# The inverses of an RWKV-7 mixer: whole 128x128 blocks, or packed 64x64 diagonal blocks and a corner by two products

## The reference

```python
def step(S, inp):
    w_t, k_t, v_t, kk_t, a_t = inp[:5]
    S = (S * w_t[:, :, None, :]
         - jnp.einsum('bhvk,bhk->bhv', S, kk_t)[..., None] * (kk_t * a_t)[:, :, None, :]
         + v_t[..., None] * k_t[:, :, None, :])
    return S, (jnp.einsum('bhvk,bhk->bhv', S, inp[5]) if emit else None)
```

## Time and profile before

| | |
|---|---|
| median of 3 runs | 3352.41 us (3349.59 to 3357.58) |
| the profiled execution | 3355.02 us |
| its span in the profile | 3353.3 us |
| mean granted clock of TensorE | 0.975 |
| instructions in the span | 46356 |
| busy: PE, DVE, ACT, POOL | 3154.9, 2226.6, 1367.8, 215.9 us |

### The profile page before, as it was taken

The page is one execution under the profiler, slowest core; times in us unless marked ns, Lnnn a source line. Parts: engine busy times, 40 slices in busy tenths (PEclk is TensorE's granted clock), DMA queues, the critical chain, the costliest instruction groups (busy, mean ns, idle before and its releaser), DMA issues.

```text
span 3353.3 us, 46356 instructions
## 1 busy us (share of the span) xinstructions
PE 3154.9 (94%) x18816; PEld 2644.4 (79%) x18816; DVE 2226.6 (66%) x2767; ACT 1367.8 (41%) x1654; POOL 215.9 (6%) x394
## 2 busy tenths in 40 slices
PE   5899999779999999889999999989989899999999
PEld 2588988448888888678888888889877788888887
DVE  2677767477777776457778778758985555555554
ACT  1322311365555555334434444434453343434342
POOL 1000000000000000001212121100000000000000
PEclk9899999889999999799999999999999999999999
DMA  9977987870000021458888888855404555555553
GB/s 324 356 259 248 323 281 246 301 273 11 12 13 12 12 52 24 148 164 285 290 284 291 293 287 296 272 183 183 164 1 138 164 189 188 192 196 186 192 188 126
DMA packets 306001, 640.88 MB, mean 191 GB/s; under 512 B 19035, under 2 KB 23937, under 8 KB 303585
## 3 DMA queue, kind: packets, MB, share of 16 engines
q1 hardware_dynamic: 269280, 529.94, 46.9%
q0 software_dynamic: 28384, 94.76, 8.6%
q10 hardware_dynamic: 8128, 13.24, 1.1%
HBM read 624.33 MB, written 13.40 MB: 190 GB/s over the span
## 4 chain that ended last, share of the span: by engine, by line
PE 86%; DVE 7%; DMA 3%; ACT 2%; issue 1%; ACTq 0%; SPq 0%; POOLq 0%; DVEq 0%
PE ps L441 45%; PE ps L459 14%; PE ps L461 7%; PE ps L1549 6%; DMA raw<-in_ada_w_dram 3%; PE ps L1592 3%; PE ps L2210 2%; PE ps L378 1%; PE ps L1646 1%; PE ps L1603 1%; DVE rw_scl L1269 1%; DVE rw_scc L1272 1%; PE ps L1481 1%; DVE line L748 1%; PE ps L1616 1%
## 5 line engine op out<-in xcount | busy, mean ns | idle before, releaser
L406 ACT ACTIVATE split_hi<-raw 128x2048 fp32r<-128x2048 f32 x368 | 702.2, 1912 | 1176.6 <-PE ps L441 838.1
L418 DVE TENSOR_TENSOR split_lo<-raw,split_hi 128x2048 fp32r<-128x2048 f32 (+1 forms) x372 | 849.7, 2285 | 500.3 <-ACT split_hi L406 490.5
L459 PE MATMUL ps<-xa,split_hi 128*128 128x512 f32 x2048 | 723.5, 398 | 6.5 <-ACT xa L613 6.5
L461 PE MATMUL ps<-xa,split_lo 128*128 128x256 f32 x2048 | 574.0, 280 | 0.0
L459 PEld LDWEIGHTS ps<-xa,split_hi 128*128 128x128 f32 x2048 | 384.7, 188 | 103.1 <-ACT xa L613 7.4
L441 PE MATMUL ps<-split_hi,hT_hi 128*128 128x512 f32 x1024 | 399.6, 390 | 0.0
L441 PE MATMUL ps<-split_hi,hT_lo 128*128 128x512 f32 x1024 | 398.5, 389 | 0.0
L441 PE MATMUL ps<-split_lo,hT_hi 128*128 128x512 f32 x1024 | 398.4, 389 | 0.0
L461 PEld LDWEIGHTS ps<-xa,split_lo 128*128 128x128 f32 x2048 | 386.5, 189 | 0.2
L441 PEld LDWEIGHTS ps<-split_hi,hT_hi 128*128 128x128 f32 x1024 | 192.2, 188 | 41.5 <-issue 1.8
L441 PEld LDWEIGHTS ps<-split_hi,hT_lo 128*128 128x128 f32 x1024 | 192.2, 188 | 40.3
(11 more groups left out here) (367 smaller groups left out, 4868.8 us busy)
## 6 DMA issues: line engine op xcount, KB each, us to landing
raw<-in_mlp_w_dram SPq DMA_DIRECT2D x256, 1024.0 KB, 5.4
raw<-in_ada_w_dram SPq DMA_DIRECT2D x64, 1024.0 KB, 9.5
raw<-in_mix_in_w_dram SPq DMA_DIRECT2D x48, 1024.0 KB, 5.9
raw<-in_conv_pw_w_dram SPq DMA_DIRECT2D x48, 1024.0 KB, 5.2
gate<-in_ada_w_dram SPq DMA_DIRECT2D x172, 256.0 KB, 4.9
line<-in_ada_w_dram POOLq DMA_DIRECT2D x171, 256.0 KB, 5.0
late<-in_ada_w_dram POOLq DMA_DIRECT2D x85, 256.0 KB, 5.1
tmpa<-in_ada_w_dram SPq DMA_DIRECT2D x84, 256.0 KB, 4.9
```

The costliest lines, as they stand in the source:

```text
L406: nc.scalar.activation(split_hi[:, c, :, 0:n], raw[:, c, :, 0:n], ACT.Copy).then_inc(hi_done, 1)
L418: nc.vector.tensor_tensor(split_lo[:, c, :, 0:n], raw[:, c, :, 0:n], split_hi[:, c, :, 0:n], ALU.subtract).then_inc(lo_done, 1)
L459: pe.matmul(ps[:, base + j, :], split_hi[:, c, kk, j * P:(j + 1) * P], both, start=(k == 0), stop=False, skip_group_check=True)
L461: mm = pe.matmul(ps[:, base + j, 0:SEQ], split_lo[:, c, kk, j * P:(j + 1) * P], xa_hi[:, k, :], start=False, stop=(k == KT - 1), skip_grou ...
```

## The change

The seven levels become six, on the 64x64 blocks of the diagonals alone. Each 128x128 matrix has two such blocks, one on the upper 64 partitions and one on the lower. The blocks of two chunks, eight on either half, are packed into one tile `zz[:, b]` of 128x512 (b = 0 for the two context chunks, b = 1 for the latent ones), by two ACT copies of 64 partitions each (`packed`). A product of the identity with `zz` opens the accumulation in PSUM (`opened`). Then each level, for each of the two tiles: DVE masks straight out of PSUM (`masked`), PE turns the sixteen 64x64 blocks by products with a 64x64 identity (`turn_mask`), ACT copies them (`turned_masks`), and sixteen 64x64 products add to the same PSUM bank (`update`). ACT's `level_values` copies the level's sum to `zz` for the next product. PE's order is turn 0, corners, opening 1, update 0, and then turn k, update k for k from 1 to 9; turns 10 and 11 and updates 10 and 11 close it.

The off-diagonal 64x64 block of each inverse, its corner, comes from two products. The corner of the score matrix is made again in the other orientation by PE from `kx` and `bh` (`corners`) and copied by ACT with a minus sign. `opened_corner` puts the corner itself into PSUM, `corner_half` adds its product with one diagonal inverse, `corner_turn` turns the other, and `corner` adds the last product in the scan, after the first chunk's `inputs_of`. ACT and DVE copy one direction's corners each into `tt`. `tt` is cleared once ahead of the first pass, since half of each matrix stays zero. Semaphores are merged, the epilogue's steps on DVE move to other places among the fewer masks, and `shift_value` moves behind the inverse's last copies.

The core of the diff:

```diff
-LEVELS = 7
+LEVELS = 6
+HB = P // 2
...
-            late("mb", P, 2, 4, P)
-            late("mx", P, 2, 4, P)
+            late("mb", P, 2, 8, HB)
+            late("mt", P, 2, 8, HB)
+            late("zz", P, 2, 8, HB)
             late("tt", P, 4, 4, P)
-            late("rh", P, 4, HD)
-            late("u", P, 4, HD)
+            late("ru", P, 2, 4, HD)
             late("sp", P, 2, 2, HD)
             late("o", P, SEQ)
+        t["rh"], t["u"], t["nt"] = t["ru"][:, 0, :, :], t["ru"][:, 1, :, :], t["ru"]
+        t["zt"], t["gz"] = t["mb"][:, :, 0:4, :], t["mb"][:, :, 4:8, :]
...
-        ZB, MB = [0, 1, 2, 3], [6, 7]
-        NS = 4 * LEVELS
-        SCB = [7, 2, 6, 0, 1, 3, 7, 2, 6, 0, 7, 1, 2, 3, 1, 2]
+            "cum_ps", "cum", "v", "prod", "tr_ps", "tr", "sc_ps", "sc", "mb", "mb0", "mbt_ps", "mt_a", "z_lev", "zz", "off_ps", "off_a", "off_d", "th", "th1",
+            "rh_ps", "rh", "u_ps", "u", "o_ps", "o", "st_ps", "sp", "epi_ps", "om", "sqo", "pr",
+            "g_ps", "y", "bv", "khd")}
+        ZB, MB, GB, NTB = [0, 3], [7, 4], [6, 2], [1, 2]
+        NT_DVE = 2 * (LEVELS - 1)
+        NS = 2 * LEVELS
+        SCB = [7, 2, 6, 0, 1, 3, 4, 7, 2, 6, 1, 3, 4, 7, 2, 6]
+        late_half = lambda d: slice((1 - d) * HB, (2 - d) * HB)
+        own_half = lambda d: slice(d * HB, (d + 1) * HB)
+        def pair_scores(b):
+            return rw["scl"] if b else rw["scc"]
...
+            def packed(x, b):
+                act.wait_ge(W["sc"], x.n(16, 8 * b + 8))
+                for e in range(2):
+                    h = own_half(e)
+                    ins = nc.scalar.activation(rw["zz"][h, b, :, :].rearrange("p (i c) s -> p i c s", c=2),
+                                               pair_scores(b)[h, :, :, h].rearrange("p c i s -> p i c s"), ACT.Copy)
+                ins.then_inc(W["zz"], 1)
+            def corners(x, h):
+                act.wait_ge(W["off_ps"], x.n(8, h + 1))
+                nc.scalar.activation(rw["nt"][:, h, :, :], ps[:, NTB[h], 0:4 * HB].rearrange("p (c s) -> p c s", c=4), ACT.Copy,
+                                     scale=-1.0).then_inc(W["off_a"], 1)
+            def level_values(x, k):
+                act.wait_ge(W["mb"], x.n(NT_DVE, k + 1))
+                nc.scalar.activation(rw["zz"][:, k % 2, :, :], ps[:, ZB[k % 2], :].rearrange("p (j s) -> p j s", s=HB), ACT.Copy).then_inc(W["zz"], 1)
+            def turned_masks(x, k):
+                b = k % 2
+                act.wait_ge(W["mbt_ps"], x.n(NS, k + 1))
+                nc.scalar.activation(rw["mt"][:, b, :, :], ps[:, MB[b], :].rearrange("p (j s) -> p j s", s=HB), ACT.Copy).then_inc(W["mt_a"], 1)
+            def own_blocks(x, b):
+                act.wait_ge(W["z_lev"], x.n(NS, NS - 1 + b))
+                for e in range(2):
+                    h = own_half(e)
+                    ins = nc.scalar.activation(rw["tt"][h, 2 * b:2 * b + 2, :, h].rearrange("p c i s -> p i c s"),
+                                               ps[h, ZB[b], :].rearrange("p (i c s) -> p i c s", c=2, s=HB), ACT.Copy)
+                ins.then_inc(W["zz"], 1)
+            def half_product(x, b):
+                act.wait_ge(W["off_ps"], x.n(8, 3 + 2 * b))
+                nc.scalar.activation(rw["gz"][:, b, :, :], ps[:, GB[b], 0:4 * HB].rearrange("p (j s) -> p j s", s=HB), ACT.Copy).then_inc(W["off_a"], 1)
+            def corner_out(x, b):
+                act.wait_ge(W["off_ps"], x.n(8, 7 + b))
+                nc.scalar.activation(rw["tt"][own_half(1), 2 * b:2 * b + 2, 2:4, late_half(1)].rearrange("p c i s -> p i c s"),
+                                     ps[own_half(1), GB[b], 0:4 * HB].rearrange("p (i c s) -> p i c s", c=2, s=HB), ACT.Copy).then_inc(W["off_a"], 1)
             def inverse(x):
-                for k in range(NS):
-                    act.wait_ge(W["z7_ps"], x.n(NS, k + 1))
-                    nc.scalar.activation(rw["tt"][:, k % 4, :, :], four(ZB[k % 4]), ACT.Copy).then_inc(W["z7"], 1)
-                    n = k + 2
-                    if 4 <= n < NS:
-                        act.wait_ge(W["mbt_ps"], x.n(NS, n + 1))
-                        nc.scalar.activation(rw["mx"][:, n % 2, :, :], four(MB[n % 2]), ACT.Copy).then_inc(W["mx"], 1)
+                packed(x, 0)
+                packed(x, 1)
+                turned_masks(x, 0)
+                corners(x, 0)
+                corners(x, 1)
+                turned_masks(x, 1)
+                for k in range(NT_DVE):
+                    level_values(x, k)
+                    turned_masks(x, k + 2)
+                own_blocks(x, 0)
+                own_blocks(x, 1)
+                half_product(x, 0)
+                half_product(x, 1)
+                corner_out(x, 0)
+                corner_out(x, 1)
...
             def masked(x, k):
-                lev, c = k // 4, k % 4
-                if k < 4:
-                    dve.wait_ge(W["sc"], x.n(16, 4 * c + 4))
-                    src = scores_of(c)[:, :, 0:P]
+                lev, b = k // 2, k % 2
+                m = bc(rw["lmask"][:, lev, :, :], 4)
+                out = rw["mb"][:, b, :, :].rearrange("p (d j) s -> p d j s", d=2)
+                if lev == 0:
+                    dve.wait_ge(W["zz"], x.n(NS + 2, k + 1))
+                    V.tensor_tensor(out, rw["zz"][:, b, :, :].rearrange("p (d j) s -> p d j s", d=2), m, ALU.mult).then_inc(W["mb0"], 1)
                 else:
-                    dve.wait_ge(W["z7"], x.n(NS, k - 3))
-                    src = rw["tt"][:, c, :, :]
-                if k >= 2:
-                    dve.wait_ge(W["mbt_ps"], x.n(NS, k - 1))
-                V.tensor_tensor(dh(rw["mb"][:, k % 2, :, :]), dh(src), bc(rw["lmask"][:, lev, :, :], 2), ALU.mult).then_inc(W["mb"], 1)
-
-            def with_unit(x, k):
-
-                dve.wait_ge(W["mbt_ps"], x.n(NS, k + 1))
-                if k >= 2:
-                    dve.wait_ge(W["z7_ps"], x.n(NS, k - 1))
-                V.tensor_tensor(rw["mx"][:, k % 2, :, :], four(ps[:, MB[k % 2], :]), idb, ALU.add).then_inc(W["mx0"], 1)
+                    dve.wait_ge(W["z_lev"], x.n(NS, k - 1))
+                    V.tensor_tensor(out, ps[:, ZB[b], :].rearrange("p (d j s) -> p d j s", d=2, s=HB), m, ALU.mult).then_inc(W["mb"], 1)
+            def turned_blocks(x, b):
+                dve.wait_ge(W["off_ps"], x.n(8, 4 + 2 * b))
+                V.tensor_copy(rw["zt"][:, b, :, :], ps[:, MB[b], 0:4 * HB].rearrange("p (j s) -> p j s", s=HB)).then_inc(W["off_d"], 1)
+            def corner_out(x, b):
+                dve.wait_ge(W["off_ps"], x.n(8, 7 + b))
+                V.tensor_copy(rw["tt"][own_half(0), 2 * b:2 * b + 2, 0:2, late_half(0)].rearrange("p c i s -> p i c s"),
+                              ps[own_half(0), GB[b], 0:4 * HB].rearrange("p (i c s) -> p i c s", c=2, s=HB)).then_inc(W["off_d"], 1)
...
                 masked(x, 0)
...
                 mask_scores(x, 3)
...
+                for k in range(1, NS):
                     masked(x, k)
                     if not first:
...
+                        if k == 1:
+                            group_scale(x.last(), 0)
+                            group_scale(x.last(), 1)
+                        elif k == 2:
                             normalised(x.last())
...
+                        elif k == 3:
                             affine(x.last())
...
+                        elif k == 4:
                             with_bonus(x.last())
...
+                        elif k == 5:
                             gated(x.last())
...
+                    if k == 6:
                         bonus_sum(x)
...
+                    elif k == 7:
                         bonus_product(x)
...
+                    elif k == 8:
                         chunk_decays(x)
...
+                    elif k == 9:
                         bonus_values(x)
                     if not last:
...
+                        if k == 9:
                             dve.wait_ge(W["pr"], x.n(1, 1))
                             current(x.next())
...
+                        elif k == 10:
+                            shift_key(x.next(), 0)
+                            shift_query(x.next(), 0)
+                        elif k == 11:
+                            shift_key(x.next(), 1)
+                            shift_query(x.next(), 1)
+                if not last:
+                    shift_key(x.next(), 2)
+                    shift_query(x.next(), 2)
+                turned_blocks(x, 0)
+                turned_blocks(x, 1)
+                corner_out(x, 0)
+                corner_out(x, 1)
+                if not last:
+                    dve.wait_ge(W["bv"], x.n(1, 1))
+                    for part in range(3):
+                        shift_value(x.next(), part)
...
+            steps.link(V.memset(rw["tt"][:, :, :, :], 0.0))
...
+            def opened(x, b):
+                pe.wait_ge(W["zz"], x.n(NS + 2, b + 1))
+                free_of_scores(x, ZB[b])
```

(86 more changed lines are left out.)

91 lines of the change are left out of this document (25 added, 66 removed).

## The result

The changed kernel takes 3364.29 us (median of 7 runs, 3361.47 to 3367.81), the kernel before 3354.07 (7 runs on the same chip): a ratio of 1.0032 with an interval of 1.002 to 1.0045, some 10 us slower. The profiled execution took 3361.91 us, 6.9 more than that of before. First the page of the changed kernel: its span, and busy us with the share of the span and the instructions by engine.

What follows compares the result with a forecast made beforehand. PE's stream was taken to bound the inverse. Steady passes +1.2, first -1.6, last +0.8 and memset +1.8 gave +2.2 on the profiled 3355.0, which stood 2.6 above the median: 3355 us on the median, range 3335 to 3600.

Steps and rivals of the forecast that it cites:

- the case that had the most weight: Whole kernel: full clock, halved products gaining nothing per level because PE pauses for copies; 3355 us, chance 0.48.
- the low clock in the loop: Inverse's loop: granted clock falls to 0.50, +23 us a pass, 3540 us in all; chance 0.35.
- The step of a pair: Turns and updates: two 64x64 products on opposite corners side by side, 0.058 us a pair, between 0.055 and 0.064.
- The loop's period: Inverse's loop: 32 pairs in 2.07 us plus ACT's copy with handoffs, 0.67, make 2.74; nine periods 24.7.
- four changes of the array's form: Inverse's loop: 0.1 us each, an estimate that no profile row prices alone.
- The head: Before the loop: packing behind the square root and the opening before chunk 3's scores start the first update 3.3 us later.
- The tail: Last update to the first product with the inverse: some 5.5 us instead of 2.8; from update 9's start 10.6.
- A steady pass: Six middle passes of the mixer: +0.2 us each, +1.2 together, 77.3 us a pass.
- The first pass: No square root ahead of packing, chunk 3's masks sooner: -1.6 us; clearing tt ahead of the first keys: +1.8.
- The last pass: Mixer's last pass: no rates to run beside rh, some half of their 1.06 us more: +0.8.
- The clock: Mixer's windows: granted clock 1.00, or 0.50 with pairs 0.107 us apart; the low clock had chance 0.35.
- POOL's loads have time to spare: Value shift after the inverse: loads for the following pass wait some 10 us longer, with most of a pass to spare.

Runs made afterwards that it cites:

- e1_pairs: Changed kernel with only PE's order altered: from k = 2, turns k and k+1 are issued, then updates k and k+1; 3310.85 us, 0.9872 of the kernel before.
- e3_head: Changed kernel with the first tile packed ahead of ACT's square root and its opening product behind chunk 3's scores; 3343.22 us, 0.9967 of the kernel before.
- e8_filled_only: Changed kernel plus two useless PE products in the heads, ahead of the first tile's opening; 3360.98 us, 1.0019 of the kernel before.
- e6_all: e1_pairs plus e3_head's head with earlier turn 0 copy and update 0, diagonal copies shared by ACT and DVE, shifts behind mask 9; 3276.28 us, 0.9767.
- e2_one_corner: Changed kernel with all eight products of the array's upper corner issued, then all eight of the lower, instead of alternating; 3543.59 us in one run.
- e5_filled: e1_pairs plus two useless PE products in the heads, ahead of the first tile's opening; 3306.76 us, 0.9855 of the kernel before.
- e4_tail: Changed kernel with the diagonal blocks' copies shared by ACT and DVE and the scan's first inputs between the tiles' corner products; 3362.0 us, 1.0028.
- e9_gate_scan: e6_all with POOL's gate-row loads moved from pass 7's inverse to pass 7's own scan; 3271.91 us, 0.9754 of the kernel before.
- e7_gate_late: e6_all with POOL's gate-row loads moved from pass 7's inverse to the last pass's scan; 3284.74 us, 0.9797 of the kernel before.

## Why the prediction was right, and where its sums were off

The likelier side, slower, came, by the case that had the most weight: full clock in the loop, pairs side by side, a pause at every step. That the side came out right is in part luck. This case put the kernel at 3355, no change, and gave slower only 0.16 of its 0.48; most of the 0.56 for slower was the low clock in the loop, at 3540, which did not come. The mechanism is what the traces bear out; the 10 us come from a sum that was mis-sized, and from dips of the clock and a stall that no term had.

- **The step of a pair.** Predicted 0.058, between 0.055 and 0.064. Rows of 64 instructions in e1_pairs take 1.86 to 1.88 us for 32 pairs: 0.058. The state products by columns and the 64x64 row by geometry had bracketed it.
- **The loop's period.** Predicted 2.74, measured 2.78: the copy with its handoffs was 0.67 as taken from the earlier trace rows, the products 2.11 in place of 2.07. The nine periods of the sum make 0.3 to 0.4 us of the pass's surplus. The gates, the bonus and the rows right behind them take 2.17 in the chain where the sum had 2.0: 1.6, and 0.1 for each of four changes of the array's form, a figure that no run shows.
- **The head.** First update 3.3 us later predicted; it starts 20.38 into the pass where it was 17.16, so 3.2. e3_head showed the reason to be the one given, the packing behind the square root and chunk 3's scores behind the opening.
- **The tail.** From the last update's end to the first product with the inverse 5.5 predicted; the timelines give 5.65. Update 9's start to there: 10.70 against 10.6.
- **A steady pass.** The sum was +0.2; +0.83 came. This term was mis-sized: 0.45 of the 0.63 lie between the first update and update 9 (28.05 us against 27.6), 0.1 in the tail. Small differences of large terms: loop, head and tail were each right within 3%, and their sum was off by a factor of four.
- **The first pass.** Predicted +0.2 (-1.6 and +1.8 for the memset). The memset took 1.76, but the keys start 2.23 later for it; the head lost 1.72 instead of 3.2 for want of the square root, 1.5 less where 1.8 was predicted. With the steady pass's surplus that is some 1.6, and +1.40 came.
- **The last pass.** The first product with the inverse is 1.19 later (predicted 0.8); then the scan is 2.6 us shorter, since the clock stayed up until 1356.8, 63.8 us into the pass, where it fell 58.3 into the pass before. That gain was in no term, and it belongs to the execution as much as to the change: from the first product with the inverse to the mean of the outputs the same scan takes 25.2 us here, 26.3 in e8_filled_only and 20.1 in e6_all (27.7 before).
- **The clock.** The prediction said 1.00 in the mixer's windows, or else a fall in the loop. The loop held 1.00 (e2_one_corner's did not). Twice the clock fell in the head instead, 3.4 us each time for 1.65 us a pass; I had costed the head's longer wait but not looked at it as a place where the clock could fall. e8_filled_only and e5_filled show the cause, no dip in fourteen heads, and the passes' windows the price.
- **Pass 7.** It is 0.73 longer than the other steady passes, all of it between update 9 and the end of update 11, at a stall inside a row, which the prediction had no term for. I had written that POOL's loads have time to spare, and thought of their landing only.

Six steady passes at 0.83, the dips 3.3, the first pass 1.4, pass 7's 0.73 and the last pass's -1.4 make the table's 9.0. The medians are 10.2 us apart, the two traced executions 6.9; where the rest lies isn't shown, as the other executions have no trace.

## What to carry to other kernels

Packing two small products onto the corners of the array cut PE's time for a level from 5.32 to 3.74 us, but only with an order that keeps PE fed: with two tiles in flight, issue both tiles' turns and then both tiles' updates, so that each copy lies under the other tile's row. When work on the bounding engine shrinks, look first for what has been hiding under it: here the copies, the packing, the inputs, the loads and the clock all came out. A small net effect that is the difference of terms of 30 us each is worth little as a forecast, and much as a list of places to work at.

## What the runs showed of the hardware that was not expected

- **The clock falls in some passes and not in others with the same work ahead.** Of the seven heads from pass 2 on, two had a dip in the changed kernel, four each in e1_pairs and e2_one_corner, five in e4_tail, none in the kernels where PE waits less there. What decides between passes isn't shown.
- **PE can stand inside a row of products with no wait.** This is the row of the changed kernel's pass 7, on PE's timeline:

```profile
1265.59 0.97 PE L1662 MATMUL ps<-ident_t,rw_mb 64*64 64x64 f32 x26 [0.51 <-issue]
```

Such stalls, up to 2.1 us, stand in pass 7 of five of the kernels, beside the gate rows' loads; the kernel before, e2_one_corner, e4_tail and e8_filled_only have none there in spite of the same loads. Where the loads moved, two shorter ones are left: 0.57 in the last pass of e9_gate_scan, beside the last of the loads, and 0.43 in pass 5 of e7_gate_late, with no load near. The loads are thus neither enough nor always needed. The Trainium skill, page "Runtime: NRT & Kernel Launch", section "Instruction fetch mechanics", says that an engine fetches its instructions by DMA in blocks and that this is usually hidden. The traces fit a block that came late. Their DMA packets have a queue for instructions (q8), and in the mixer one block of 16 KB starts to move on it for every 256 products and weight loads of PE on average. Of all eleven traces, each of the eight blocks that started latest, 363 to 440 of these instructions after the one before, has a stall of 0.2 to 2.1 us behind it, and so have three of the thirty that started 320 to 361 after. PE went on 0.9 to 1.5 us after the block had landed, and ten of these eleven blocks started while a load of the gate rows was moving. The loop of e1_pairs goes through 594 products and 592 weight loads in 19 us, 310 of each in 35.3 us before, so it needs a block every 4.1 us. No run delayed the blocks alone, so the cause is likely, not proven.
- **Dips and stalls weigh as much as an edit of half a per cent.** e3_head gained 21 us for 14 expected, e4_tail 2 for 10, e5_filled 4 for 8, and in each the passes' windows show a dip or a stall more or less. For such edits a steady pass of the trace told more than the whole time.
